# First tile's modulation moved behind its turning, and a second buffer for the second tile's h in the second sweep

## What is computed

```python
def rms_norm(x, g):
    return x * lax.rsqrt(jnp.mean(x * x, -1, keepdims=True) + EPS) * g
# per layer
shift1, scale1, gate1, shift2, scale2, gate2 = split(silu(c) @ w_ada + b_ada, 6)
h = rms_norm(x, norm1_g) * (1 + scale1) + shift1
u, v_a, q, k, v_b, gates = split(h @ w_in)
...                                  # mixer A (gated MLP), mixer B (window attention)
g_a, g_b = split(sigmoid(gates))
x = x + gate1 * ((g_a * (out_a @ w_pa) + g_b * (out_b @ w_pb)) @ w_o)
h2 = rms_norm(x, norm2_g) * (1 + scale2) + shift2
...                                  # two of 32 experts for each token, then a last rms_norm
```

## Time and profile before

| What | Value |
|---|---|
| runs, median of three | 1897.4 us |
| profiled execution, own time | 1899.67 us |
| its span, first to last instruction | 1898.0 us |
| PE busy | 1830.8 us, 96% of the span |
| DVE, ACT, POOL busy | 60%, 38%, 12% |
| mean granted clock of PE | 0.981 of full speed |

### The profile page before, as it was taken

One profiled execution on the slowest core, in us unless ns is written; L12 is line 12 of the kernel. 1 busy time (PEld: TensorE's weight loads), 2 busy tenths in 40 slices (PEclk: granted clock), 3 DMA queues, 4 the chain that ended last, 5 costly groups with the idle time before them and its releaser, 6 DMA issues.

```text
span 1898.0 us, 29695 instructions
## 1 busy us (share of the span) xinstructions
PE 1830.8 (96%) x9077; PEld 1381.1 (73%) x9078; DVE 1137.9 (60%) x2171; ACT 727.8 (38%) x1356; POOL 229.4 (12%) x331
## 2 busy tenths in 40 slices
PE   5999999999999999999899999999899999999987
PEld 2787778777567777777588888888477777777632
DVE  3788888888540000001655555556778888888648
ACT  3444444434330000002321221221477777777522
POOL 0100000000000000000101111101322222222111
PEclk7999999999899999999999999999999999999998
DMA  9322212222485444455844344444889869999587
GB/s 373 108 95 112 108 70 106 112 97 91 181 271 192 177 177 177 177 188 185 307 161 151 133 155 144 155 147 166 273 281 354 292 213 337 328 355 313 193 334 316
DMA packets 175851, 384.40 MB, mean 203 GB/s; under 512 B 30184, under 2 KB 104056, under 8 KB 168572
## 3 DMA queue, kind: packets, MB, share of 16 engines
q1 hardware_dynamic: 139836, 321.28, 47.8%
q0 software_dynamic: 19744, 53.89, 7.6%
q10 hardware_dynamic: 16224, 8.65, 1.5%
HBM read 296.80 MB, written 103.73 MB: 211 GB/s over the span
## 4 chain that ended last, share of the span: by engine, by line
PE 66%; DVE 3%; DMA 2%; issue 1%; ACT 1%; ACTq 0%; POOL 0%; DVEq 0%; SPq 0%; POOLq 0%
PE bank L168 18%; PE bank L170 17%; PE bank L169 17%; PE bank L2865 4%; PE bank L2830 2%; PE bank L2008 2%; PE bank L2970 1%; DMA mixer_parts<-oT_split 1%; PE bank L1307 1%; PE bank L2068 1%; DVE late_x L2807 1%; PE bank L2853 1%; DVE expert_down L2802 0%; DMA gathered<-weighted_rows 0%; DMA expert_down<-weighted_rows 0%
## 5 line engine op out<-in xcount | busy, mean ns | idle before, releaser
L168 PE MATMUL bank<-w_mix_hi,hT_hi 128*128 128x512 f32 (+3 forms) x544 | 203.2, 374 | 3.8 <-DVE hT_lo L610 2.5
L1216 DVE SCALAR_TENSOR_TENSOR ma_rows<-tanh_rows,bank 128x512 f32<-128x512 f32 x32 | 20.6, 684 | 310.2 <-PE bank L170 159.9
L2728 DVE TENSOR_TENSOR gate_up_lo<-expert_gate_up,gate_up_hi 128x2048 fp32r<-128x2048 f32 x86 | 196.4, 2288 | 10.9 <-ACT gate_up_hi L2588 9.9
L169 PE MATMUL bank<-w_mix_hi,hT_lo 128*128 128x512 f32 (+3 forms) x544 | 198.8, 365 | 0.0
L170 PE MATMUL bank<-w_mix_lo,hT_hi 128*128 128x512 f32 (+3 forms) x544 | 198.3, 365 | 0.0
L2588 ACT CAST gate_up_hi<-expert_gate_up 128x2048 fp32r (+1 forms) x86 | 165.1, 1923 | 69.0 <-issue 67.2
L168 PE MATMUL bank<-gate_up_hi,gathered_T_hi 128*128 128x512 f32 x352 | 142.5, 405 | 4.9 <-DVE gathered_T_lo L2719 2.1
L170 PE MATMUL bank<-gate_up_lo,gathered_T_hi 128*128 128x512 f32 x352 | 138.4, 393 | 0.0
L169 PE MATMUL bank<-gate_up_hi,gathered_T_lo 128*128 128x512 f32 x352 | 137.9, 392 | 0.0
L168 PEld LDWEIGHTS bank<-w_mix_hi,hT_hi 128*128 128x128 f32 (+1 forms) x544 | 100.6, 185 | 37.0 <-issue 20.3
L170 PEld LDWEIGHTS bank<-w_mix_lo,hT_hi 128*128 128x128 f32 (+1 forms) x544 | 100.6, 185 | 19.1
(11 more groups left out here) (463 smaller groups left out, 3833.9 us busy)
## 6 DMA issues: line engine op xcount, KB each, us to landing
expert_gate_up<-in_w_gate SPq DMA_DIRECT2D x33, 1024.0 KB, 9.6
expert_gate_up<-in_w_up SPq DMA_DIRECT2D x33, 1024.0 KB, 13.1
expert_down<-in_w_down SPq DMA_DIRECT2D x32, 1024.0 KB, 12.7
h_parts<-hT_split SPq DMA_DIRECT2D x16, 1024.0 KB, 5.1
mixer_parts<-oT_split SPq DMA_DIRECT2D x32, 512.0 KB, 8.2
w_ada_part<-in_w_ada SPq DMA_DIRECT2D x16, 1024.0 KB, 10.7
h_parts_b<-hT_split SPq DMA_DIRECT2D x16, 1024.0 KB, 4.9
expert_down<-weighted_rows SPq DMA_DIRECT2D x12, 1024.0 KB, 8.2
```

What stands on the lines that cost most here:

```text
L168: nc_mm(out, left[0], right[0], start=first, stop=False)
L169: nc_mm(out, left[1], right[0], start=False, stop=False)
L1216: last = nc.vector.scalar_tensor_tensor(out=ma[:, par, at], in0=tg[:, at], scalar=1.0, in1=ps[2 + n][:, :], op0=ALU.add, op1=ALU.mult)
L2728: nc.vector.tensor_tensor(wg[par][1][:, at], ring[:, bass.ds(slot * GU + n * HG, HG)], wg[par][0][:, at].bitcast(F32), ALU.subtract).then_ ...
```

## The change

Two parts. In the first sweep x of tile 1 and the six short rows are loaded after the third slice of w_ada. DVE multiplies x by the reciprocal root mean square alone, and PE turns it after the sixth slice's product. Scale and shift are made into columns, 16 in all, one for each block of 128 columns: each is a product of a 32 by 128 block of the ada rows with one column of `chosen`. DVE copies the 16 columns out of bank 2. The turned blocks are multiplied by their scale column and get their shift column as they leave the banks: four on ACT, four on DVE, into `first_hT` (the shift half of `mod`). ACT casts from there and DVE subtracts from there, in one instruction of 1024 columns. The spread products stay, for the later tiles, and move behind the columns. On ACT slice 1 of w_mix moves behind the first tile.

In the second sweep h of tile 2 gets a buffer `second_h`, which lies where `attn_out` and `h_b` lie later. Its load no longer waits for `gated` 2, but for the last stores of the sweep before and for the first h; it stands ahead of the `mod_b_sample` pieces. The load of h of tile 3 comes behind them; it waits for h of tile 2 to land (`h_in` 32) and `gated` 2. POOL now waits for `h_in` 48, which is the landing of h of tile 3. DVE's first write to `attn_out` waits for `gated` 3. One step of SP's loop is written out.

```diff
+        mod_columns = tiny[:, 8:8 + 2 * KD]
+        first_hT = mod[:, 1, :].rearrange("p (k m) -> p k m", m=P)
...
             for k in range(KD):
                 sp.dma_start(slices[k], a["w_ada"][0, k * P:(k + 1) * P, 0:2 * D]).then_inc(ada_in[k], 16)
-            sp.dma_start(x[:, :], a["x_prompt"][0, 0:P, :]).then_inc(x_in, 16)
...
+                if k == 2:
+                    sp.dma_start(x[:, :], a["x_prompt"][0, 0:P, :]).then_inc(x_in, 16)
+                    biases()
...
+            def first_high():
+
+                act.wait_ge(d_norm, 1)
+                act.wait_ge(h_turned, 1)
+                for k in range(KD // 2, KD):
+                    last = nc.scalar.activation(first_hT[:, k, :], ps[1][:, (k % 4) * P:(k % 4 + 1) * P], ACT.Identity,
+                                                scale=mod_columns[:, KD + k:KD + k + 1], bias=mod_columns[:, k:k + 1])
+                last.then_inc(modulated, 1)
+                for n in range(2):
+                    act.wait_ge(modulated, 2)
+                    last = nc.scalar.copy(hT[0][:, 4 * n:4 * n + 4, :], first_hT[:, 4 * n:4 * n + 4, :])
+                last.then_inc(hi_ready, 1)
...
             act.wait_ge(ada_summed, 1)
-            for k in range(2):
-                high_w(k)
-            high(0, P, True)
+            high_w(0)
+            first_high()
+            high_w(1)
...
+            dve.wait_ge(rrms, 1)
+            nc.vector.tensor_scalar(x[:, :], x[:, :], tiny[:, 2:3], None, ALU.mult).then_inc(h_ready, 1)
             dve.wait_ge(bias_in, 16 * 6)
             dve.wait_ge(ada_summed, 1)
...
-            dve.wait_ge(rrms, 1)
-            for n in range(2):
-                dve.wait_ge(spread, n + 1)
...
+            dve.wait_ge(columns, 4)
+            nc.vector.tensor_copy(mod_columns, ps[2][:, 0:2 * KD]).then_inc(d_norm, 1)
             dve.wait_ge(d_norm, 1)
...
+            dve.wait_ge(h_turned, 1)
+            for k in range(KD // 2):
+                last = nc.vector.tensor_scalar(first_hT[:, k, :], ps[0][:, k * P:(k + 1) * P], mod_columns[:, KD + k:KD + k + 1],
+                                               mod_columns[:, k:k + 1], ALU.mult, ALU.add)
+            last.then_inc(modulated, 1)
             low_w(0)
-            low(0, P)
+            dve.wait_ge(hi_ready, 1)
+            nc.vector.tensor_tensor(hT[1][:, :, :], first_hT, hT[0][:, :, :].bitcast(F32), ALU.subtract).then_inc(lo_ready, 1)
...
+                if k == 5:
+                    turn_h(0, P, True)
             last.then_inc(ada_summed, 1)
-            pe.wait_ge(ada_rows, 2)
             pe.wait_ge(zeroed, 8)
+            for j in range(4):
+                rows = slice(32 * j, 32 * j + 32)
+                pe.wait_ge(ada_rows, 1 if j < 2 else 2)
+                if j:
+                    pe.wait_ge(columns, j)
+                for k in range(4):
+                    last = nc.tensor.matmul(ps[2][:, 4 * j + k:4 * j + k + 1], ada[rows, k * P:(k + 1) * P], chosen[rows, j, 0:1], start=True, stop=True,
+                                            tile_position=(32 * j, 0))
+                last.then_inc(columns, 1)
...
-            turn_h(0, P, True)
             tile(0, P, True)
...
-            load_h(2)
             sp.wait_ge(shared["stored_ma"][0], 16 * (NT // 2 + 1))
             sp.wait_ge(shared["stored_pb"][0], 16 * (NT // 2 + 1))
+            sp.wait_ge(h_in, 16)
+            load_h(2, second_h)
...
+            sp.wait_ge(h_in, 32)
+            sp.wait_ge(gated, 2)
+            load_h(3)
             load_m(2)
             sp.wait_ge(filled, 48)
...
-            pool.wait_ge(h_in, 32)
+            pool.wait_ge(h_in, 48)
...
                 if m == MS:
                     dve.wait_ge(raw_used, 2 * KW)
+                    dve.wait_ge(gated, 3)
...
+                left = second_left if isinstance(i, int) and i == 2 else h_left
+                product(0, left, 0).then_inc(gated, 1)
```

More of the change, by code:

```diff
@@ L285, in _, with biases @@
         def _(sp):
+            def biases():
+                sp.wait_ge(zeroed, 4)
+                for j in range(4):
+                    rows = slice(32 * j, 32 * j + R)
+                    sp.dma_start(ada[rows, :], a["b_ada"][0:1, j * 512:(j + 1) * 512].to_broadcast([R, 512])).then_inc(bias_in, 16)
+                    if j >= 2:
+                        sp.dma_start(gains[rows, :], a["norm1_g"][0:1, (j - 2) * 512:(j - 1) * 512].to_broadcast([R, 512])).then_inc(bias_in, 16)
             sp.dma_start(c_rows[0:1, :], a["c_prompt"]).then_inc(c_in, 16)
@@ L565, in _ @@
                     part, j = ((0, 2), (0, 3), (1, 0), (1, 1))[n]
-                    act.wait_ge(d_norm if n < 2 else h_ready, 1)
+                    act.wait_ge(spread, 4)
+                    if n >= 2:
+                        act.wait_ge(lo_ready, 1)
                     nc.scalar.copy(mod[:, part, (j % 2) * 512:(j % 2 + 1) * 512], ps[4 + j][:, :]).then_inc(mod_ready, 1)
@@ L1348, in gate_b @@
         h2T = sb("h2_T", [P, D])
+        with nc.sbuf_tensor("second_h", [P, 2 * D], F32R) as second_h:
+            pass
         xo = sb("attn_out", [P, D])
@@ L1436, in slice_in, with load_h @@
                 sp.dma_start(raw(k), src).then_inc(raw_in[k], 16)
-            def load_h(i, first=False):
-                if not first:
-                    sp.wait_ge(gated, i)
+            def load_h(i, place=hb):
                 src = s["hT"][bass.ds(i - 1, 1), :, :].rearrange("o p c -> p (o c)")
-                sp.dma_start(hb[:, :].bitcast(F32), src).then_inc(h_in, 16)
+                sp.dma_start(place[:, :].bitcast(F32), src).then_inc(h_in, 16)
             def load_m(i, first=False):
@@ L1487, in on_sync @@
             load_x(1)
-            with sp.Fori(1, NT - 1) as i:
+            load_m(3)
+            stores(1)
+            load_x(2)
+            with sp.Fori(2, NT - 1) as i:
+                sp.wait_ge(gated, i + 2)
                 load_h(i + 2)
@@ L2003, in gate @@
                 pe.wait_ge(tanhed, i)
-                product(0, h_left, 0).then_inc(gated, 1)
+                left = second_left if isinstance(i, int) and i == 2 else h_left
+                product(0, left, 0).then_inc(gated, 1)
             def turn(i, m, src, bank, done):
```

27 lines of the change are left out of this document (7 added, 20 removed).

## The result

The changed kernel took 1905.14 us (median of seven runs, 1901.99 to 1908.75) against 1899.13 for seven runs of the kernel before (1896.42 to 1900.05). The ratio is 1.0038, with a 95% interval of 1.0026 to 1.0050: slower by 0.38%, or 5 to 9.5 us. The forecast was slower by 4.2 us (1901.6, range 1895.8 to 1904.5). The sign held; the time lies 0.6 us above the range. The forecast was counted from 1897.4, the median of three runs of the kernel before; all seven beside the changed kernel have a median 1.7 higher, and as a difference the 6.0 us are inside what the range allows (1.6 faster to 7.1 slower). But neither term of the sum had its size: the gain of the first part didn't come at all, and the loss of the second was smaller than forecast.

What follows compares the result with a forecast made beforehand. PE, busy 96% of the span, was taken as the bound, so only its idle or low-clock stretches count. First tile -2.7 and gate_b +6.9 gave +4.2 us: 1897.4 + 4.2 = 1901.6 us, range 1895.8 to 1904.5.

Steps and rivals of the forecast that it cites:

- the gain of the first part: First tile: PE's first w_mix product at 36.5 instead of 39.25, 2.7 us gained, bounds 1.0 and 3.9.
- the loss of the second: gate_b: output product of tile 1 4.8 us later, plus 2.1 lost to the clock, together 6.9 us slower.
- 1.4 for the columns: First tile: of four groups of column products, two run beside DVE's second operation and two behind it, costing 1.4 us.
- The third rival: First tile: PE stays at the low clock through slices seven and eight; gain only 1.1, total +5.8 (1903.2), chance 0.20.
- the slow landing: gate_b: upper bound, output product of tile 1 5.5 us later if the landing is slower, where 4.8 was taken.
- No gain from the early issue: gate_b: h of tile 2, issued earlier, keeps its place in SP's queue and gains 0 us, bound -3.
- the rival of an early landing: gate_b: the queue doesn't hold h of tile 2 back; total -1.3 us (1896.1), chance 0.12.
- Nothing else in the fill is changed: gate_b: POOL's fill starts 4.8 us later, is otherwise unchanged, and lands at 946.0 instead of 941.2.
- The second rival: gate_b: with h early, the fill takes some 7 us instead of 11.0; total -7.4 us (1890), chance 0.08.
- The clock term: gate_b: output product of tile 1 starts at the low clock after PE's idle stretch, losing 2.1 us, bounds 0 and 2.5.
- The fourth rival: gate_b: the clock holds through the idle stretch before the output product; total +2.1 us (1899.5), chance 0.15.
- two waits end together: gate_b: the late gate product of tile 2 (ends 942.8) and ACT's wait for the fill (941.22) both precede the output product.

Runs made afterwards that it cites:

- part1_alone: Changed kernel with only the first-tile part kept, gate_b as in the kernel before: 1899.24 us against 1898.94 for the kernel before, ratio 1.0000.
- part1_cols4: Only the first-tile part of the change, its sixteen columns made by four products over 128 rows: 1895.73 us against 1898.33 for the kernel before, ratio 0.9986.
- whole_again: The changed kernel unedited, measured once more: 1904.48 us against 1898.05 for the kernel before, ratio 1.0032.
- fill32: Changed kernel with POOL waiting for h of tile 2 again, not tile 3: 1903.13 us against 1898.94 for the kernel before, ratio 1.0021.
- h_ahead48_late: Changed kernel, h of tile 2 queued ahead of mod_b, ACT's fill wait moved behind the cast of tile 1: 1897.13 us against 1898.07 before, ratio 0.9993.
- cols4_h_later: Changed kernel, columns by four products, h of tile 2 ahead of mod_b, ACT's, SP's and POOL's fill waits moved later: 1890.59 us against 1898.05 before, ratio 0.9955.
- h_ahead48: Changed kernel with the load of h of tile 2 ahead of mod_b in SP's queue: 1905.32 us against 1898.33 for the kernel before, ratio 1.0040.
- late_wait: Changed kernel with ACT's wait for the fill moved behind the cast of tile 1: 1900.18 us against 1898.07 for the kernel before, ratio 1.0016.
- h_ahead32: Changed kernel, h of tile 2 ahead of mod_b, POOL waiting for h of tile 2 only: 1899.58 us against 1898.33 for the kernel before, ratio 1.0009.

## Why the prediction was wrong, point by point

**First part: the step that failed is the columns.** The sum had 30.4 for the ada rows, 1.4 for the columns, 0.25 for the copy, 1.1 for the operations on blocks, 2.0 and 1.3 for DVE's slice and subtraction, and PE at 36.5. Measured: ada rows at 29.74 (the seventh and eighth slice went at the high clock here, as taken, and the last slice came at 27.13, not 27.75); copy at 34.54, so 4.80 us for the columns; from there to PE's product 4.75 us, where 4.65 had been counted. The 3.4 us that the columns took more, less the 0.7 by which the ada rows came earlier, are the whole 2.7 of gain; none of it came, outside the bounds of 1.0 to 3.9. The bound that I had taken from the pair of 128x1 products, 0.5 to 1.2 for a group, does hold the 1.17 measured at the high clock. The mistake was to let two groups run beside DVE's second operation, which takes 0.69 us: they need 2.3 there, and the two behind it another 2.3 at least. The sum also had no term for a clock that falls during the columns: three groups began 1.17 us apart here, the fourth went at the low clock, at which a group took 1.98 in part1_alone. That the price lies in the passes, and in the waits between groups, is shown by part1_cols4: with eight passes in place of 32, and one group, PE began at 36.02, and the time fell by 2.6 us.

The third rival (little gain, as PE stays at the low clock for the last slices) had the right outcome for the wrong stretch in the first profile, and half the right stretch in whole_again (the seventh slice took 1.94 there, the eighth 1.09). With the slow landing its sum gives 1903.9, not the 1904.5 at which the range ends.

**Second part: mechanism right, its terms partly mis-sized.** "No gain from the early issue" held to 0.05 us: h landed at 929.64, after 14.80 us in place of 10.6. That the queue ordered it is shown by h's place in it: behind `mod_b` it took 14.0 to 15.7 us from issue to landing in six profiles, ahead of it 9.1 to 11.0 in six. So the rival of an early landing fell. The Trainium skill (DMA: Bandwidth & Descriptors, section Queues, rings and completion order) has each DMA engine consume a ring's descriptors in ring order; these runs agree.

The fill began 6.1 us later (4.8 forecast, as h of tile 3 took 6.04 rather than 4.7 to 5.0), but took 8.6 instead of 11.05. "Nothing else in the fill is changed" was the wrong sentence: what runs beside it was (0.06 MB of SP's loads in place of 1.11). The second rival's short fill was half true, then, behind the late start. So the output product came 3.64 later, not 4.8. The clock term was 2.1. The tenth product of the output, after and before:

```profile
951.06 0.40 PE L168 MATMUL bank<-w_out_hi,merged_T_hi 128*128 128x512 f32 x1
```

```profile
945.85 0.39 PE L168 MATMUL bank<-w_out_hi,merged_T_hi 128*128 128x512 f32 x1
```

It starts 3.70 us after the first where it took 2.13 before: some eight products at the low clock, 1.6 us. The fourth rival (no clock lost there) fell in this profile; in that of fill32 it would have held. Part two: +5.2 in place of +6.9.

**The rest.** The two add up to 5.2 for the profiled execution, which took 6.6 more. The other 1.4 are products at the low clock at the start of the experts (from 1391 us). Such a stretch is there in three other profiles too (fill32 at 1391, h_ahead48_late at 1384, cols4_h_later at 1377) and not in that of before or in the rest; it goes with no edit. The Trainium skill (TensorE: Matmul & The Clock Gate, Part 1) says that the point at which the clock changes varies. The profiles agree: of two of the changed kernel one has this stretch and one has not. That the sum came within 2 us of the measured 6.0 is in part luck: a gain that didn't come was set off by a loss that was counted too large.

**What both parts had in common.** The prediction said that two waits end together in gate_b, and that who removes one meets the other. h_ahead48 shows it: 4.0 us less at one, 6.8 more at the other. But the prediction took ACT's wait for the fill as given. It is placed a tile ahead of what it protects: late_wait got 3 to 4 us back with the fill as late as in the changed kernel (POOL begins it at 936.14). That SP's and POOL's waits for the fill held time too is shown by cols4_h_later for both together, not for each.

## What to carry to other kernels

Price small products by passes, each with its own weight load (0.11 us at the high clock, 0.21 at the low one, with 0.25 to 0.3 us between dependent groups), and put several columns into one pass (four cost no more than one here). A load that is issued earlier landed no earlier here while the queue ahead of it was full: look at what is queued, and reorder that; but what is moved back in the queue comes later, and may be waited for in its turn. And where a transfer holds three engines, look for each at what the wait protects: to move one wait back got 3 to 4 us back here, nearly as much as to move two transfers forward (4 to 6 in h_ahead32), and the fastest version has both sorts of edit.

## What the runs showed of the hardware that was not expected

- Eight passes of 128x4 over 128 rows took 1.03 us, eight of 32x1 over 32 rows 1.02.
- One 1 MB load took 10.6 and 14.8 us to land at about the same moment, issued 4.2 us apart behind the same queue; ahead of 1.5 MB of that queue it took 9.1 to 11.0.
- The same 2.4 MB fill took 8.6, 11.05 and 13.2 us, with 0.06, 1.11 and 2.13 MB loaded beside it.
- PE's clock can fall in the middle of a row of small products that PE works through almost without a gap (granted 0.61 and 0.50 of full speed from 30 to 34 and 34 to 38 us in part1_alone, PE busy 3.55 and 3.75 of 4 us). Before it fell PE had waited 1.03 us for a slice of w_ada and 0.97 for the ada rows.
